# Second pass's tokens numbered by a small product, the samples' second norm on GpSimd and ScalarE, a split load of constants

## The reference

```
x = layer_norm(ALPHA * x + ctx @ p['ca_wo'], p['ln2_g'], p['ln2_b'])
g_sel = jnp.argmax(g_logits, -1)
e_in = jnp.take_along_axis(e_logits, g_sel[:, None, None], axis=1)[:, 0]
top_p, top_i = lax.top_k(jax.nn.softmax(e_in, -1), TOP_K)
gate = jnp.take_along_axis(pg, g_sel[:, None], 1) * top_p / top_p.sum(-1, keepdims=True)
e_idx = g_sel[:, None] * EXPERTS_PER_GROUP + top_i
hh = jax.nn.silu(hg) * hu * combine[..., None]
y = jnp.einsum('nef,efd->nd', hh, p['w_down'])
x = layer_norm(ALPHA * x + hier_moe(x, p), p['ln3_g'], p['ln3_b'])
```

## Time and profile before

| what | us |
|---|---|
| median of 3 runs (lowest, highest) | 697.22 (695.97, 698.03) |
| the profiled execution's own time | 699.21 |
| its span, first to last instruction | 696.9 |
| busy: PE, DVE, POOL, ACT | 662.7, 290.9, 197.9, 158.2 |

### The profile page before, as it was taken

How to read it: one execution, slowest core, us unless ns; L and a number is a source line. 1 busy time by engine, 2 the same in 40 slices (tenths; PEclk the granted TensorE clock), 3 DMA queues, 4 the chain that set the end, 5 groups by cost and what they waited for, 6 DMA issues and landing times.

```text
span 696.9 us, 8496 instructions
## 1 busy us (share of the span) xinstructions
PE 662.7 (95%) x3250; PEld 395.9 (57%) x3250; DVE 290.9 (42%) x698; ACT 158.2 (23%) x349; POOL 197.9 (28%) x233
## 2 busy tenths in 40 slices
PE   6999999999999999999999999999889999999884
PEld 3445688745887774446896774444564444333241
DVE  0280030005457792745000865356863342434345
ACT  1113232101334230001110740222313111111124
POOL 4240010000476466412000895103335221110101
PEclk9999999999999999999999999999979999999998
DMA  8984414123335345004940687544618999999366
GB/s 294 385 294 158 136 37 145 35 86 122 94 95 177 104 151 185 16 0 166 380 149 13 237 300 300 204 185 163 244 60 320 416 417 415 399 387 407 117 261 120
DMA packets 44503, 142.40 MB, mean 204 GB/s; under 512 B 5464, under 2 KB 5528, under 8 KB 40359
## 3 DMA queue, kind: packets, MB, share of 16 engines
q1 hardware_dynamic: 32663, 111.73, 42.5%
q0 software_dynamic: 9744, 25.30, 11.4%
q10 hardware_dynamic: 2056, 4.82, 1.9%
HBM read 130.30 MB, written 17.08 MB: 211 GB/s over the span
## 4 chain that ended last, share of the span: by engine, by line
PE 87%; DVE 5%; DMA 3%; ACT 2%; issue 1%; POOL 1%; ACTq 0%; SPq 0%; DVEq 0%; POOLq 0%
PE ps L403 28%; PE ps L636 12%; PE ps L928 12%; PE ps L436 8%; PE ps L948 6%; PE ps L993 2%; PE ps L732 2%; PE ps L661 2%; PE ps L546 1%; PE ps L716 1%; PE ps L911 1%; PE ps L561 1%; DMA wring<-in_ca_wk 1%; PE ps L645 1%; PE ps L464 1%; DMA P<-in_cache_mem_v 1%
## 5 line engine op out<-in xcount | busy, mean ns | idle before, releaser
L403 PE MATMUL ps<-xT,wring 128*128 128x312 f32 (+1 forms) x768 | 170.4, 383 | 0.3 <-ACT xT L1175 0.3
L403 PEld LDWEIGHTS ps<-xT,wring 128*128 128x128 f32 x768 | 139.9, 190 | 28.9 <-issue 1.1
L636 PE MATMUL ps<-wring,P 128*128 128x512 f32 x224 | 99.2, 596 | 0.0
L636 PEld LDWEIGHTS ps<-wring,P 128*128 128x128 f32 x224 | 41.6, 190 | 49.1 <-issue 49.0
L928 PE MATMUL ps<-wring,P 128*32 128x512 f32 (+1 forms) x288 | 65.8, 602 | 1.7 <-DVE P L1944 0.9
L436 PE MATMUL ps<-wring,P 128*128 128x512 f32 x128 | 57.9, 611 | 0.7 <-DMA wring<-in_ca_wk 0.6
L2066 POOL TENSOR_SCALAR rstd<-agg 128x1 f32<-128x1 f32 (+1 forms) x15 | 16.8, 1120 | 112.0 <-DVE agg L1494 111.9
L928 PEld LDWEIGHTS ps<-wring,P 128*32 128x32 f32 (+1 forms) x288 | 22.5, 131 | 37.3 <-issue 37.3
L436 PEld LDWEIGHTS ps<-wring,P 128*128 128x128 f32 x128 | 24.8, 196 | 31.3 <-issue 30.1
L1199 ACT ACTIVATE P<-ps 128x312 f32<-128x312 f32 (+1 forms) x40 | 15.5, 388 | 118.4 <-PE ps L403 118.4
L1944 DVE COPY P<-ps 128x512 f32<-128x512 f32 x11 | 7.6, 692 | 82.0 <-PE ps L911 82.0
(11 more groups left out here) (358 smaller groups left out, 944.6 us busy)
## 6 DMA issues: line engine op xcount, KB each, us to landing
wring<-in_w_in SPq DMA_DIRECT2D x5, 2048.0 KB, 8.6
wring<-in_w_gate SPq DMA_DIRECT2D x10, 1024.0 KB, 10.6
wring<-in_w_up SPq DMA_DIRECT2D x10, 1024.0 KB, 14.6
P<-in_w_down SPq DMA_DIRECT2D x10, 1024.0 KB, 12.7
P<-in_cache_mem_k SPq DMA_DIRECT2D x8, 1024.0 KB, 6.0
P<-in_cache_mem_v SPq DMA_DIRECT2D x8, 1024.0 KB, 5.0
wring<-in_ca_wv SPq DMA_DIRECT2D x2, 2048.0 KB, 20.1
wring<-in_w_out SPq DMA_DIRECT2D x2, 2048.0 KB, 10.3
```

What stands on the lines that cost most here:

```text
L403: last = mm(out, lhs(k), rhs(k), start=(k == 0), stop=(k == n - 1))
L636: last = mm(bk[:, :], src[:, k, START[t]:START[t] + TR], w[:, k, :], start=(k == 0), stop=(k == KC - 1))
```

## The change

1. **Start.** The load of the constants is split: `ident` (64 KB) first, the rest (401 columns, 205 KB) only after ACT's two copies of the turned memory rows. SP loads the second half of the memory rows after the four quarters of `wk0`. PE turns the first half only, starts `memory_block("wk0", 0)`, and turns the second half inside it, ahead of its sixth k (`between`).
2. **The samples' second norm.** DVE adds and takes statistics before it touches tile 4. POOL computes the root and minus mean times root (`samples_rstd`, four operations), ACT applies scale and bias, and POOL multiplies by the gain and adds the offset (`samples_affine`, 8x1024 each). A semaphore of its own (`x2_samples`) tells PE and ACT.
3. **Two selection matrices.** `list_rows` becomes `pick_slots` (slot and mask of expert 0 and of expert 4, and a selection matrix for each) and `name_slots` (`dst`). For the samples and tile 4, both `pick_slots` come ahead of `gates` and `name_slots`.
4. **Pass 1's tokens by a product.** PE's `pick_tokens` multiplies expert 4's selection matrices with a column of token numbers (five products with one column each), DVE adds an offset into `idx1`, and `gather(1)` reads `idx1`. It stands ahead of the last two `scatter_lists` and no longer waits for the lists.
5. **Order on PE.** `count_choices(2)` goes into the last `rows_project`, at k = 6, whose middle no longer holds the samples' transposes; those, `pick_rows(0)` and `pick_rows(1)` come before, around and after `router(SAMPLES)`. One of the five `keep_running` products stands behind `transpose_x(4)`.

One of the two gathers has moved ahead of the last four scatters; the other still follows the loaded lists. The core of the diff:

```diff
-            for m in range(2):
-                pe.wait_ge(act_free, m + 1)
-                pe.wait_ge(dve_free, m + 1)
-                memory_block("wk0", m)
+            turn_memory(0, (bank_a(), bank_d()))
+            second = (bank_a(), bank_d())
+            pe.wait_ge(act_free, 1)
+            pe.wait_ge(dve_free, 1)
+            memory_block("wk0", 0, lambda: turn_memory(1, second))
...
+            def pick_tokens():
+                pe.wait_ge(picks_ready, 2 * NT)
+                bk = bank_d()
+                for t in range(NT):
+                    n = rows_of(t)
+                    last = mm(bk[:, 0:1], picks[0:n, 1, t, :], con[0:n, 524 + t:525 + t], start=(t == 0), stop=(t == NT - 1))
+                last.then_inc(dve_full, 1)
...
-            rows_project(4, WC[1:2], ctxT, lambda: transpose_x(SAMPLES, x2_ready))
+            counts_bank = bank_d()
+            rows_project(4, WC[1:2], ctxT, lambda: count_choices(2, counts_bank), 6)
...
-                V.tensor_tensor(r[:, 95:96], r[:, 40:41], r[:, 56:57], ALU.add).then_inc(pick_known, 1)
+                mask, slot = r[:, 96:98], r[:, 98:100]
+                V.tensor_tensor(mask, r[:, 40:48:4], r[:, 56:64:4], ALU.add)
                 dve.wait_ge(dve_free, nf[0])
-                dve.wait_ge(pick_known, n + 1)
-                V.tensor_scalar(picks[0:rows, n, :], slots16[0:rows, :], tmp[:, 0:1], r[:, 95:96], ALU.is_equal, ALU.mult)
+                link(V.tensor_tensor(slot, tmp[:, 0:8:4], con[0:rows, 320:328:4], ALU.subtract))
+                for e in range(2):
+                    V.tensor_scalar(picks[0:rows, e, n, :], slots16[0:rows, :], slot[:, e:e + 1], mask[:, e:e + 1], ALU.is_equal, ALU.mult).then_inc(picks_ready, 1)
...
-            list_now(SAMPLES)
-            list_now(4)
+            pick_slots(SAMPLES)
+            pick_slots(4)
+            bk = full()
+            V.tensor_scalar(idx1, bk[:, 0:1], float(NOROW), None, ALU.add).then_inc(dve_free, 1)
+            at["second tokens"] = nf[0]
+            for n in (SAMPLES, 4):
+                gates(n)
+                name_slots(n)
...
+            samples_rstd()
             scatter_lists(0)
-            norm_rstd(SAMPLES)
+            samples_affine()
             scatter_lists(1)
             norm_rstd(4)
-            for n in range(2, NT):
+            scatter_lists(2)
+            pool.wait_ge(x2_out, 16 * NT)
+            pool.wait_ge(dve_free, at["second tokens"])
+            gather(1)
+            for n in range(3, NT):
                 scatter_lists(n)
...
-            pool.wait_ge(x2_out, 16 * NT)
-            for p in (1, 2):
-                gather(p)
+            gather(2)
```

More of the change, by code:

```diff
@@ L265, in layer_kernel @@
         flag = sb("flag", [1, 1], I32)
+        idx1 = smp[:, 2455:2456].bitcast(U32)
         turn = smp[0:1, 1001:1005]
@@ L317, in layer_kernel @@
         sum_full, row_parts = sem("sum_full"), sem("row_parts")
-        sortc_in, chosen_ready, idx2_ready, pick_known = [sem(s) for s in ("sortc_in", "chosen_ready", "idx2_ready", "pick_known")]
+        sortc_in, chosen_ready, idx2_ready = [sem(s) for s in ("sortc_in", "chosen_ready", "idx2_ready")]
         lists_in = [sem(f"lists_in{i}") for i in range(3)]
@@ L430, in memory_block @@
                 for k in range(KC):
+                    if k == 5 and between:
+                        between()
                     if name == "wk0" and m == 0 and k % 2 == 0:
@@ L466, in transpose_x @@
                 at["x2 rows", t] = na[0]
[L468 to L471 removed]
+            turn_memory(0, (bank_a(), bank_d()))
[3 more added lines that the diff above has]
+            memory_block("wk0", 0, lambda: turn_memory(1, second))
+            pe.wait_ge(act_free, 2)
+            pe.wait_ge(dve_free, 2)
+            memory_block("wk0", 1)
             for m in range(2):
@@ L626, in _, with rows_project @@
             at["pool"] = na[0]
-            def rows_project(t, names, src, between=None):
+            def rows_project(t, names, src, between=None, step=KC // 2):
                 for name in names:
@@ L633, in rows_project @@
                     for k in range(KC):
-                        if k == KC // 2 and between:
+                        if k == step and between:
                             between()
@@ L827, in pick_rows, with spare @@
                     for j in range(4):
-                        last = mm(ps[6 + q][:, j * C:j * C + C], xturn[0:n, t, 4 * q + j, :], picks[0:n, t, :], start=False, stop=(t == NT - 1 and j == 3))
-                    if t == NT - 1:
+                        last = mm(ps[6 + q][:, j * C:j * C + C], xturn[0:n, t, 4 * q + j, :], picks[0:n, 0, t, :], start=False, stop=(t == 4 and j == 3))
+                    if t == 4:
                         last.then_inc(xgT_full, 1)
+            def pick_tokens():
+                pe.wait_ge(picks_ready, 2 * NT)
+                bk = bank_d()
+                for t in range(NT):
+                    n = rows_of(t)
+                    last = mm(bk[:, 0:1], picks[0:n, 1, t, :], con[0:n, 524 + t:525 + t], start=(t == 0), stop=(t == NT - 1))
+                last.then_inc(dve_full, 1)
+            def spare():
+                pe.wait_ge(act_free, na[0] - 2)
+                return RING_A[na[0] % 3]
             def keep_running(bank, n):
@@ L1722, in residual_samples, with sample_statistics @@
                 link(V.scalar_tensor_tensor(x, x, ALPHA, mixed_rows if rows == "mixed rows" else cross_rows, ALU.mult, ALU.add))
-                norm(SAMPLES, signal)
+            def sample_statistics():
+                statistics(SAMPLES, 0)
+                link(statistics(SAMPLES, 1))
+                pows[0] += 1
+                V.bn_aggr(agg_samples[:, 0:2], st_samples[:, :]).then_inc(var_ready, 1)
             dve.wait_ge(gb_in, 32)
@@ L1753, in _ @@
             residual(4, x1_ready)
-            residual_samples("mixed rows", x1_ready)
+            residual_samples("mixed rows")
+            norm(SAMPLES, x1_ready)
             NQ = NQT * 4
@@ L1897, in _ @@
             list_now(0)
-            residual(4, x2_ready, between=(lambda: residual_samples("cross rows", x2_ready), lambda: list_now(1),
-                                           lambda: take_logits(2), lambda: choose_now(2)), meanwhile=lambda: gates(2))
+            residual_samples("cross rows")
+            sample_statistics()
+            residual(4, x2_ready, between=(lambda: list_now(1), lambda: take_logits(2), lambda: choose_now(2), lambda: list_now(2)))
             take_logits(SAMPLES)
-            list_rows(2)
             choose_now(SAMPLES)
@@ L2210, in _, with gather @@
             pool.wait_ge(tok_ready, 6)
+            def gather(p):
+                s = p % 3
+                if p >= 3:
+                    pool.wait_ge(xgT_full, 2 * (p - 2))
+                if p > 1:
+                    pool.wait_ge(*entry_landed(p))
+                index = idx1 if p == 1 else entry(p)[:, 0:1].bitcast(U32)
+                pool.indirect_dma_start(out=xg[:, s, :], out_offset=None, in_=x2_d, bounds_check=NTOK - 1, oob_is_err=False,
+                                        in_offset=bass.IndirectOffsetOnAxis(ap=index, axis=0)).then_inc(xg_in[s], 16)
             def scatter_lists(n):
```

111 lines of the change are left out of this document (69 added, 42 removed).

## The result

The changed kernel takes 710.92 us (median of four runs, 710.15 to 713.01), the kernel before 697.33 (695.97 to 698.03): a ratio of 1.0202, 95% interval 1.0175 to 1.0229, 14 us slower. The profiled execution took 713.01 us with a span of 711.1, against 699.21 and 696.9 before, so the two traces show the same 14 us. The forecast was 1 us faster.

The account below looks back on a forecast made before the run. PE, busy 95% of the span, was taken as the bound, with few breaks to move. Terms -0.6 (start), -3.9 and -2.5 (picks, pass 0), +3.7 (gather), +2.3 (clock) gave -1.0 us: 696.2 from 697.22, range 690.0 to 699.8.

Parts of the forecast that it names:

- Start, -0.6: First memory block: first product at 8.2, 2.0 us earlier, less the eight transposes moved inside; gain 0.6 us (-0.9 to 1.1).
- Samples' norm: Samples' second norm: 3.4 us off DVE, about 4.5 us on POOL; norm 4 at 499.5, last choice 1.3 us earlier.
- Picks, -3.9: Sample and tile 4 picks: pass 0 starts at about 514.3 instead of 518.21, 3.9 us earlier (2.0 to 4.5).
- Pass 0, -2.5: Pass 0: with the clock staying up it takes 6.9 to 7.1 us instead of 9.40, gaining 2.5 us.
- Gather(2), +3.7: Pass 2's tokens: the gather takes 8.3 us in the weights' traffic, lands at 533.7, and PE stands 3.7 us.
- the lists 2.4 us later: List loading before gather(2): lists at 521.8, 2.4 us behind the last scatter at about 519.3.
- 0.6 for the lists' own loading: Before gather(2): 0.6 us allowed for loading the lists in the weights' traffic.
- Rival (c): Pass 2's gather is late, slower than before: 14.0 us, landing at 539.4, +4.4 us in all, 701.6; chance 0.15.
- The aside on an even share of the DMA engines: Gather(2) with half the traffic: landing of about 6.5 us, PE's wait 1.3 us shorter; not used in the sum.
- Clock behind the wait, +2.3: After PE's wait for gather(2): the clock may fall, costing 0 to 4.6 us, taken as 2.3.
- norm 4 ended after 500.5: Sign in tile 4's norm: if it ends after 500.5, the forecast of POOL's part is wrong.
- pass 0 came after 516: Sign at pass 0's start: if it comes later than 516, the forecast of the picks' part is wrong.

Follow-up runs that it names:

- a4_one_input: Changed kernel with POOL's two two-input operations on the sample rows made one-input, gain and offset left out; 708.09 us, 1.0158 of the kernel before.
- d10_two_matrices: Kernel before with only the two selection matrices and pass 1's tokens by a product, list places named ahead of token numbers; 693.15 us, 0.9982.
- before_again: The kernel before, unchanged, run for a second trace; 1.0010 against itself.
- a6_pool_order: Changed kernel with only POOL's order changed: the last four scatters stand ahead of pass 1's gather; 704.65 us, 1.0156 of the kernel before.
- c7_norm_back: `a3_names_first` with the samples' second norm back on DVE, inside tile 4's residual; 699.24 us, 1.0083 of the kernel before.
- a2_weights_wait: Changed kernel where SP's weight loads from the fourth expert on also wait for gather(2); 705.49 us, 1.0149 of the kernel before.
- a3_names_first: Changed kernel with POOL's last scatters ahead of gather(1), and DVE's last gates and list places ahead of token numbers; 697.66 us, 1.0022 of the kernel before.
- e13_both: Kernel before with the constants' load split, plus the two matrices and tokens by a product as in `d10_two_matrices`; 692.75 us, 0.9983.
- e16_both_wait: `e13_both` with SP also waiting for pass 2's gather before it loads the ranked weights; 696.47 us, 1.0032 of the kernel before.
- c9_no_start: `c7_norm_back` with the start of the kernel before; 698.03 us, 1.0063 of the kernel before.

## Why the prediction was wrong

1. **Start, -0.6.** The rows came as forecast (first product 8.11 for 8.2, the block's end 0.56 us earlier than in the first trace). The step that failed stood ahead of it: I took the landing of 8.38 us in one execution as the old start's time. The old start usually begins its products at 8.8 to 9.1, and then the new one is 1 to 1.5 us slower by the chains and 2 by the medians.
2. **Samples' norm.** POOL's price was right (2.34 and 2.33 for 2.26). The step "That takes two 1.27 us passes and the wait off DVE, 3.4 us in all" left out that POOL and DVE don't run side by side here: DVE gave back 1.94 and 1.73 us under the two products. PE, which was to wait 0.7 us for the samples, waited 3.78 us for tile 2's choices. Behind that wait, at the lower clock for a part of it (0.50 from 497 to 500), its work up to tile 4's transposes took 11.84 us (493.84 to 505.68), against 8.63 for the same work in `a4_one_input` (491.29 to 499.92). So norm 4 ended at 502.1 instead of 499.5, PE turned its rows only at 505.68, and the last choice came at 513.88 instead of 508.2, 5.7 us late. In the trace of `a4_one_input` it comes at 508.38; by the ratios that kernel is 3 us faster.
3. **Picks, -3.9.** The mechanism was right and is seen in `d10_two_matrices` (-3.6, clock up). In the whole change it was eaten by point 2: pass 0 at 519.69, 1.5 us later than before instead of 3.9 earlier.
4. **Pass 0, -2.5.** 7.11 for 9.40, so -2.3; with points 2 and 3, pass 0 ended 0.8 us earlier than before. But the 9.40 were one execution's as well: in `before_again` pass 0 takes 7.11 and the picks 7.21 instead of 6.24, since the lower clock lasts some 6.8 us there (509.4 to 516.2, from its windows) instead of 10.2.
5. **Gather(2), +3.7.** This is the term that decides. I forecast places at 516.6, the last scatter at 519.3, the lists' loading at 521.8, the gather at 524.8, landing at 533.7. It was 522.2, 526.34, 532.38, 538.44, 547.04, which is 13.3 us late. The places were 5.6 late through point 2, but so was PE, which wanted the rows at 535.88 instead of 530.0; this part doesn't lengthen the wait. What does is the rest: 1.4 for the scatter, which stood behind pass 1's gather and three others, then 3.5 for its landing and 3.1 for the lists, in the traffic; the gather's own 8.60 was priced well (8.3). So PE stood 11.3 us instead of 3.7. The failed step is "the lists 2.4 us later" and "0.6 for the lists' own loading": prices of quiet DMAs for transfers that by my own times ran as the weights started (I had them at 520.0 in one sentence and at 521.5 in another, the last scatter at 519.3), since the weights wait for pass 1's gather and POOL issues the last scatters behind it. Rival (c) named this ("small transfers in full traffic too") and did not price it. The aside on an even share of the DMA engines entered no sum; its landing of 6.5 us would have made the wait 1.8 us shorter, not 1.3, and the gather's 8.60 don't bear it out.
6. **Clock behind the wait, +2.3.** It was 3.0.

Measured on the chain that is -0.6 (start), -0.2 (from there to pass 0's end), then PE standing 11.3 us, with 3.0 for the clock and 0.8 at the last store of rows and its reading back: 14.2 us, the difference of the two spans. The signs that the prediction gave for being wrong appeared: norm 4 ended after 500.5, and pass 0 came after 516. Of the cases, (c) was the right one in sign and place, though not by the 14.0 us that it gave the gather. The range was too narrow because only the gather was priced as slow, and every link ahead of it was slow too. What the experiments take back is, in ratios: POOL's order 0.5%, DVE's order 1.3%; the rest of 0.2% is start, hold and PE's order against the earlier picks.

## What to carry to other kernels

- Before one transfer is moved forward, ask what its landing releases. Here it released the weights, and every small serial DMA left behind it (scatter, list, gather) cost two to three times its quiet price; such chains belong ahead of the bulk loads, and the work that feeds them ahead of anything that waits for another engine.
- An elementwise operation with two inputs that goes from DVE to POOL gave DVE no time for two-input operations of its own: they ended only with POOL's. Such a move is worth a try only where DVE has nothing of that kind to do meanwhile.
- Before a gain is computed from a start-up landing, look at a second trace of the same kernel.

## What was not expected of the hardware

- A POOL product of 8x1024 with two inputs (2.33 us) held a DVE operation with two inputs on one to sixteen columns until its own end: 0.14 to 0.24 us became 1.95 to 2.29, and a pass of 1.27 became 3.28, with POOL 0.5 us slower too. DVE's reductions issued in between took their usual 0.16 to 0.18. With one input on POOL (2.78 us) the hold was 0.35 to 0.6 us and came on three operations only, one of them (L1888, 0.86 us instead of 0.23) a TENSOR_SCALAR.
- In the weights' traffic (303 to 420 GB/s over these transfers), a scatter of list entries landed in 5.75 us against 2.14 in the quiet, the lists in 5.24 and 5.47 against 1.91 to 2.1, gathers of 512 KB in 8.6 to 11.8 against 4.32.
- TensorE's granted clock fell to the lower level behind each of the long waits (3.78 and 11.30 us here, 4.15 in `a6_pool_order`, 5.22 in `c7_norm_back`) and stayed there into the work that followed; behind 2.17 us in `a2_weights_wait` and 1.43 us in `d10_two_matrices` it stayed at 1.00. The fall that the kernel before has near 510 is absent in the traces where the picks followed the choices without a gap (the changed kernel, `a3_names_first`, `d10_two_matrices`, `e13_both`), but it is there in `e16_both_wait`, whose work up to then is that of `e13_both`, and in `c9_no_start` (0.59 from 515 to 520), where the picks had no gap either. So the gap is not all of its cause.
